# First modulation part of a two-layer diffusion backbone: features on the partitions instead of rows

## What is computed

```
def modulation(cond, w_mod, b_mod):              # w_mod: 1024 x 6144, per layer
    m = silu(cond) @ w_mod + b_mod
    return split(m, 6)                           # shift1, scale1, gate1, shift2, scale2, gate2

def adaln(h, w, shift, scale):
    return rmsnorm(h, w) * (1 + scale) + shift

ux = adaln(xs, norm1_w, sh1x, sc1x) @ w_in       # w_in: 1024 x D_IN
uc = adaln(cs, norm1_w, sh1c, sc1c) @ w_in
# pooling mixer, bidirectional SSD, grouped-query attention on parts of ux, uc
xs = xs + g1x * (concat(pool, ssd, attn) @ w_out)
xs = xs + g2x * swiglu(adaln(xs, norm2_w, sh2x, sc2x), w1, w3, w2)
```

## Time and profile before

| what | value |
|---|---|
| median of 3 runs | 1641.59 us (1641.19 to 1642.63) |
| the profiled execution's own time | 1644.12 us |
| its span | 1642.3 us |
| PE busy | 1560.3 us, 95% |
| PEld busy | 1406.5 us, 86% |
| DVE busy | 889.1 us, 54% |
| ACT busy | 594.8 us, 36% |
| POOL busy | 155.1 us, 9% |
| DMA | 154.74 MB, mean 94 GB/s |
| PE line L1734 in the chain that ended last | 68% of the span |

### The profile page before, as it was taken

The page is one execution under the profiler, slowest core; times in us unless marked ns, Lnnn a source line. Parts: engine busy times, 40 slices in busy tenths (PEclk is TensorE's granted clock), DMA queues, the critical chain, the costliest instruction groups (busy, mean ns, idle before and its releaser), DMA issues.

```text
span 1642.3 us, 22274 instructions
## 1 busy us (share of the span) xinstructions
PE 1560.3 (95%) x9042; PEld 1406.5 (86%) x9042; DVE 889.1 (54%) x1194; ACT 594.8 (36%) x902; POOL 155.1 (9%) x156
## 2 busy tenths in 40 slices
PE   6999878899999999999999999997899999999999
PEld 4899767699999999999999998996678788888887
DVE  4687775755765554555544367456565433333333
ACT  6634445543622211222112245354545422222223
POOL 0321153001000000000000023014201000000000
PEclk9999999999999999999999999998999999999999
DMA  9555100012353333333331123220003233333322
GB/s 367 165 180 177 40 1 1 1 43 74 103 168 115 128 128 128 117 115 128 128 128 55 49 77 85 65 65 1 1 28 101 77 90 102 90 92 100 90 84 82
DMA packets 203580, 154.74 MB, mean 94 GB/s; under 512 B 8612, under 2 KB 189676, under 8 KB 203372
## 3 DMA queue, kind: packets, MB, share of 16 engines
q1 hardware_dynamic: 202060, 148.85, 29.2%
q10 hardware_dynamic: 1440, 4.78, 0.8%
HBM read 151.52 MB, written 2.10 MB: 94 GB/s over the span
## 4 chain that ended last, share of the span: by engine, by line
PE 82%; DVE 10%; ACT 5%; issue 2%; POOL 0%; DMA 0%; SPq 0%; DVEq 0%; ACTq 0%
PE banks L1734 68%; PE banks L1851 6%; PE banks L2001 1%; DVE neg_max L1549 1%; PE banks L1968 1%; PE banks L1877 1%; PE banks L1945 1%; DVE w_lo L1192 1%; DVE mod_sum L1217 1%; DVE gn_r L1591 1%; DVE nrm L1294 1%; PE banks L1982 1%; DVE h_lo L1288 1%; ACT nrm L860 1%; PE banks L1686 1%
## 5 line engine op out<-in xcount | busy, mean ns | idle before, releaser
L1192 DVE TENSOR_TENSOR w_lo<-raw,w_hi 128x1056 fp32r<-128x1056 f32 x184 | 245.1, 1332 | 305.6 <-ACT w_hi L807 304.8
L1734 PE MATMUL banks<-h_hi,w_hi 128*128 128x384 f32 (+3 forms) x1296 | 387.3, 357 | 16.2 <-DVE h_lo L1288 10.4
L1734 PE MATMUL banks<-h_lo,w_hi 128*128 128x384 f32 (+3 forms) x1296 | 383.9, 354 | 0.0
L1734 PE MATMUL banks<-h_hi,w_lo 128*128 128x384 f32 (+3 forms) x1296 | 383.6, 354 | 0.0
L807 ACT ACTIVATE w_hi<-raw 128x1056 fp32r<-128x1056 f32 x184 | 198.4, 1078 | 255.2 <-PE banks L1734 228.7
L1734 PEld LDWEIGHTS banks<-h_hi,w_hi 128*128 128x128 f32 x1296 | 236.7, 189 | 44.3 <-issue 19.5
L1734 PEld LDWEIGHTS banks<-h_hi,w_lo 128*128 128x128 f32 x1296 | 238.6, 189 | 17.0
L1734 PEld LDWEIGHTS banks<-h_lo,w_hi 128*128 128x128 f32 x1296 | 238.2, 189 | 16.0
L1734 PE MATMUL banks<-g_hi,w_hi 128*128 128x384 f32 (+1 forms) x528 | 160.0, 357 | 0.0
L1734 PE MATMUL banks<-g_hi,w_lo 128*128 128x384 f32 (+1 forms) x528 | 159.1, 355 | 0.0
L1217 DVE SCALAR_TENSOR_TENSOR mod_sum<-mod_ring,cond,mod_sum 128x1024 f32<-128x1024 f32 x126 | 158.1, 1296 | 1.4
(11 more groups left out here) (208 smaller groups left out, 1946.3 us busy)
## 6 DMA issues: line engine op xcount, KB each, us to landing
raw<-in_w_dram SPq DMA_DIRECT2D x120, 512.0 KB, 3.9
mod_ring<-in_w_mod_dram SPq DMA_DIRECT2D x96, 512.0 KB, 4.9
raw<-in_w_in_dram SPq DMA_DIRECT2D x32, 512.0 KB, 5.0
raw<-in_w_out_dram SPq DMA_DIRECT2D x16, 512.0 KB, 3.7
raw<-in_w_dram SPq DMA_DIRECT2D x16, 384.0 KB, 3.2
x_in<-in_x_dram ACTq DMA_DIRECT2D x4, 512.0 KB, 8.1
out_dram<-x_out SPq DMA_DIRECT2D x8, 256.0 KB, 2.3
inv_n<-in_count_dram ACTq DMA_DIRECT2D x4, 400.0 KB, 3.1
```

Of the source, the lines that this page charges most:

```text
L1192: dve.tensor_tensor(w_lo[n % 2][:, :], raw[n % 4][:, :], as_f32(w_hi[n % 2][:, :]), ALU.subtract).then_inc(lo_ready, 1)
L1734: ins = pe.matmul(to(p, a, b), ws[:, w], xs(k, a, b), start=(first and q == 0), stop=(last and q == 2))
```

## The change

The first part in `ORDER` is multiplied with its features on the partitions. For each slab, eight matmuls take 128 columns of the slab as the weights and the two conditioning columns as the moving operand, and accumulate 128 x 2 results in bank 6, columns 2k and 2k+1. VectorE adds the bias from there in one instruction over 16 columns. The copies of its rows, its turn and the wait in front of it are gone. `row_turn` counts the remaining parts (the second is 0, and so on) and replaces `turn_of` in the counts of `rows_ready` and `rows_T`. The masks' DMA is issued behind the eighth slab of the second part, and TensorE waits for it ahead of `dense_lagged` of the first layer instead of ahead of `spread_rstd`. GpSimd's wait counts one part's rows less, and so stands for the same event.

```diff
+        row_turn = {q: k - 1 for k, q in enumerate(ORDER) if k}
...
             for kc in range(KC):
-                if kc == 2:
-                    sp.dma_start(tab[:, P:6 * P], table[:, P:6 * P]).then_inc(masks_landed, 16)
                 load_mod(ORDER[0], kc)
...
                     if l == 0 and n == 1:
                         for kc in range(KC):
                             load_mod(ORDER[1], kc)
+                        sp.dma_start(tab[:, P:6 * P], table[:, P:6 * P]).then_inc(masks_landed, 16)
...
-                    pool.wait_ge(rows_ready, 4 * 2)
+                    pool.wait_ge(rows_ready, 4 * 1)
...
-                if turn_of[q]:
-                    act.wait_ge(rows_T, turn_of[q])
+                if row_turn[q]:
+                    act.wait_ge(rows_T, row_turn[q])
...
             mean_root(0, 0)
-            mod_rows_out(ORDER[0])
             split_hi(0)
...
-                dve.wait_ge(rows_T, turn_of[l * N_MOD + part] + 1)
+                dve.wait_ge(rows_T, row_turn[l * N_MOD + part] + 1)
...
+            def first_mod_bias():
+
+                slot, before = slab_at[ORDER[0], KC - 1]
+                dve.wait_ge(mod_used[slot], before + 1)
+                v0 = V_BMOD + KC * ORDER[0]
+                dve.tensor_tensor(mods[0][:, ORDER[0], :, :], banks[:, 6, 0:2 * KC].rearrange("p (k g) -> p g k", g=2),
+                                  vecs[0][:, v0:v0 + KC].unsqueeze(1).to_broadcast([P, 2, KC]), ALU.add).then_inc(mods_ready, 2)
...
-            mod_bias(0, 1)
+            first_mod_bias()
...
-                if kc == 0 and turn_of[q]:
-                    pe.wait_ge(rows_ready, 4 * turn_of[q])
+                if kc == 0 and row_turn[q]:
+                    pe.wait_ge(rows_ready, 4 * row_turn[q])
...
+            def first_mod_step(kc):
+
+                slot, before = slab_at[ORDER[0], kc]
+                pe.wait_ge(mod_landed[slot], 16 * (before + 1))
+                for k in range(KC):
+                    ins = pe.matmul(banks[:, 6, 2 * k:2 * k + 2], mod_ring[slot][:, P * k:P * k + P], cond[:, :, kc],
+                                    start=(kc == 0 and k == 0), stop=(kc == KC - 1 and k == KC - 1))
+                ins.then_inc(mod_used[slot], 1)
...
-                pe.wait_ge(rows_ready, 4 * (turn_of[q] + 1))
-                if turn_of[q]:
-                    pe.wait_ge(mods_ready, 2 * turn_of[q])
+                pe.wait_ge(rows_ready, 4 * (row_turn[q] + 1))
+                pe.wait_ge(mods_ready, 2 * turn_of[q])
...
                 if t:
-                    mod_step(ORDER[0], t - 1)
+                    first_mod_step(t - 1)
             for kc in range(TT - 1, KC):
-                mod_step(ORDER[0], kc)
-            pe.wait_ge(masks_landed, 16)
+                first_mod_step(kc)
             spread_rstd(0, 0)
-            mod_turn(ORDER[0])
...
                 first_tiles(2 * l, base, 0, (0, 4), (0, 6), mm, None)
+                if l == 0:
+                    pe.wait_ge(masks_landed, 16)
                 dense_lagged(base + 2, h_of(h_hi), h_of(h_lo), (mm, halves(0)), (h_lo_ready, 2 * l * KC))
```

## The result

The changed kernel takes 1660.07 us (median of 4 executions, 1655.67 to 1661.55) against 1641.39 us (1640.25 to 1642.63): slower, ratio 1.0109, 95% interval 1.0089 to 1.0130, +18.7 us between the medians. The forecast was 1662.5 in a range of 1650 to 1666.

What follows compares the result with a forecast made beforehand. TensorE, busy 95% of the span, was taken as the bound. First dense matmul 22.9 us later, less 2.0 for the clock, gave +20.9: 1665.0 on the profiled execution's scale, median 2.5 lower, 1662.5 us; range 1650 to 1666.

Steps and rivals of the forecast that it cites:

- (a): New steps on TensorE: 16 load records each, 1.87 us at full clock, 3.5 at low; eight take 15 or 28 us.
- (b): Hiding of the steps: ScalarE's pace leaves 0.5 us a tile; the rest shows, and ScalarE's root is no longer waited for.
- (c): Clock during the first modulation part: low throughout, chance 0.66; last step ends at 48.6 us.
- R1: Rival: busy TensorE keeps full clock in the part; last step ends at 32.8, +4.2 us, 1645.8; chance 0.15.
- rows 7: Trace evidence at 195 us: full loads with few columns, 1.15 us idle, then granted clock 0.50 though TensorE showed busy.
- R2: Rival: clock rises once on the first tiles' transposes, then falls; 3 to 5 us saved, 1652 to 1660; chance 0.13.
- (d): Removed row copies, turn and spreading ahead: worth about 1.6 us on the old path, none of it on the new.
- (e): Clock in the first dense matmuls: shorter TensorE idle time ahead saves 2.0 us, bounds 0 and 2.9.
- (f): SyncE queue: masks' DMA moved behind the second part's eighth slab costs 0 until its landing takes over 15 us.
- R3: Rival: loads overlap, steps fit TensorE's slack at 0.84 us each; -1.6 or -4.5 us, 1640.0 or 1637.1; chance 0.04.

Runs made afterwards that it cites:

- e2: Changed kernel with the two conditioning columns repeated to 128 moving columns per matmul, same loads; 1645.57 us against 1641.63 for the kernel before, ratio 1.0025.
- e1: Changed kernel run again without edit for a second profile; 1658.63 us against 1641.63 for the kernel before, ratio 1.0102.
- e5: Changed kernel with only four of the eight matmuls per new step, half the loads; 1638.75 us against 1641.36 for the kernel before, ratio 0.9985.
- e4: Changed kernel with the old 256-column steps, their product left out, no copies or turn; 1639.89 us against 1641.63 for the kernel before, ratio 0.9988.
- e11: Kernel before plus eight unread 256-column matmuls where TensorE waits ahead of the dense work; 1639.83 us against 1641.90, ratio 0.9988.
- e3: Kernel before with only the masks' DMA and TensorE's wait for it moved; 1640.87 us against 1641.63, ratio 0.9995.
- e8: Kernel before plus eight unread 512-column matmuls where TensorE waits ahead of the dense work; 1642.33 us against 1642.91, ratio 0.9996.
- e6: Changed kernel with 128 moving columns, low half of weight tile 0 moved ahead of bias and gain; 1646.68 us against 1641.36 for the kernel before.

## Why the prediction was right

(a) The price of a load: right. 0.117 us from the sum over features is 1.78 / 16 = 0.111 in the first step of the first profile and 0.112 in e2, and 0.212 at the low clock is 3.21 / 16 = 0.20 in the steps between transposes, 3.37 / 16 = 0.21 in the run of four. I had rounded a step up to 3.5, 28.0 us for eight; in e1, all at the low clock, they take 26.45, so this was 1.6 us too much.

(b) Nothing hidden beyond ScalarE's pace: right. ScalarE waited 3.38 us a tile and stood idle for 10.6 us before the gain; the reciprocal at 32.77 was 11 us early.

(c) The clock: right in its result, and the step that carried the forecast; its reason was tested. e2 shows that with the same loads and more streaming the clock stays up, and the time is then what R1 forecast (+4.2; measured +3.9) under another kernel: R1 had the right price and the wrong condition. The rule of the Trainium skill quoted for R1 ("TensorE: Matmul & The Clock Gate", "Why this matters for your kernels") did not hold in this part: PE was busy 5.00 of 5.00 us at 0.50. But the ground I gave, rows 7, did not carry it. The clock there was still 1.00 over all of the loads and fell at about 198.9 us, behind the 1.15 us without work, so that stretch cannot tell its loads from the idle time; and e5 shows that my reading went too far, since half as many loads between the same transposes left the clock at 1.00. That the full form holds it down was shown only afterwards; to give it 0.66 on this ground was in part luck. Throughout the part was also not quite so: two of three profiles have the first step and a part of the second at a higher clock, which is R2 in small. The last step's end came at 43.8, 47.0 and 43.7 us against 48.6.

(d) The old path's worth: 1.6 us predicted, 1.7 measured in e4, and that the two agree is luck. The start moved by 1.1 us (27.83, not 27.4) because the first weight tile lands at 24.2, which the prediction had not looked at, and the clock in the dense matmuls moved as well, by 2.7 us in e4's profile. The change itself gains none of it, as said.

(e) The clock behind the part: -2.0 predicted, -2.5, -1.4 and -2.2 in the three profiles (6.10 less 3.57, 4.67, 3.95). That the 2.7 us go with TensorE's idle time ahead of them is shown by e11, where work in that time kept them.

(f) Masks and SyncE: 0 predicted and 0 in e3; in the changed kernel the masks go out at 44.16, more than 20 us ahead of the third tile.

The sum was +20.9. At the end of the first 18 dense matmuls the three profiles stand at +15.3, +19.6 and +15.5 us. For e1, low throughout as predicted, the difference is the steps (1.6 us) and the transposes between them (0.2), less 0.6 that (e) fell short. In the other two the first steps and transposes at the higher clock take off some 3.3 us more, and (e) gave a little more than 2.0. The +16.9 to +18.7 of the medians lie between these; a rest of up to 3 us lies in what varies behind 50 us, and whether the changed kernel loses more clock there on the whole is open. So the mechanism was right, and that the time came within 2.4 us of the forecast is partly this scatter.

R3 was rightly put last for this kernel: its steps cost 1.78 us at best. e5 shows that steps of 0.92 us are hidden; how much longer they could be was not tried (VectorE then still waited 1.14 us for the weight's high half).

## What to carry to other kernels

Putting the large operand on the weight side made TensorE pay 0.11 us for each load of 128 columns. The few moving columns saved nothing (1.78 us a step with 2, 1.79 with 128), and here they also cost the clock, which nearly doubled the price of the loads and of the transposes beside them. Before turning a small product round, count the loads against the slack of TensorE in that place, and look at the nearest stretch of the trace in which it does loads alone. Where such loads can't be avoided, try streaming work between or on them (e5, e2), and where TensorE must wait ahead of a dense stretch, matmuls of the right length that nothing reads can be worth their place (e11; too long in e8). Read the clock from durations as well as from its record.

## What the runs showed that I had not expected

Streaming 64 times as many columns made the part faster: 1.79 us a step against 3.21 to 3.38, at the same number of loads. The clock did not fall for the same kind of load in half the number (e5: 1.00 over 13 to 22 us), and fell when four steps stood together, with TensorE busy throughout. The chain also shows steps as serial that have a twin beside them: taking 1.17 us of VectorE's work out of the chain (e6) gained nothing, since ScalarE's high half took 1.13 beside it.
